# The same program at other SBUF addresses: buffers laid out anew, with a smaller dynamic DMA scratch

## The chip, the core and the metric

The kernel runs on one core of one Trainium2 chip. The metric is device time in microseconds (us) of one execution, and lower is better. TensorE (PE) multiplies, ScalarE (ACT) and VectorE (DVE) work elementwise, GpSimd (POOL) computes remainders here, and SyncE (SP) issues nearly all transfers. Buffers lie in SBUF, 128 partitions wide; an address below is a byte offset inside each partition. Products gather in eight PSUM banks.

## The reference, cut to what matters

A first transformer block and then two layers of a second one run on x of 512 tokens by 1024 channels, in float32.

```python
def reference(x, c, positions, w_mod, ...):
    x = first_block(x, c, positions, ...)      # modulation, gated delta rule (8 heads) and latent attention,
                                               # merged through w_o_dn, w_o_mla, w_out; then 16 experts
    return second_block(x, positions_2, ...)   # 2 layers of:

def second_block(...):
    for l in range(2):
        h = rmsnorm(x, mix_norm_g[l])
        x = x + mixing_layer(h, ...)           # short conv, differential attention, conformer conv
        h = rmsnorm(x, ffn_norm_g[l])
        x = x + swiglu(h, w_gate[l], w_up[l], w_down[l])   # hidden width 2816
    return rmsnorm(x, final_norm_g)

def expert_choice_ffn(h, ...):                 # 16 experts, 64 tokens each, hidden width 1024
    hid = silu(xe @ w_gate) * (xe @ w_up)
    ye = (hid @ w_down) * gate
```

## The kernel before

The program is one `build` function with a hand-written stream for each engine, joined by semaphores. Weights come in pieces of 1 MB, each an 8192-byte row in all 128 partitions.

**Buffers.** Nothing is allocated by a planner. `base` (line 72) is the first free SBUF byte rounded up to 64; each `Region` (from line 76) hands out offsets from `base`, one after the other, in steps of 32 bytes; `at` puts a tensor at a given offset, so that many names share one place. Ahead of the first free byte stand 97 bytes of constants and the dynamic DMA scratch, which is 16384 bytes unless the program says otherwise. So `base` is 16512, which is 8 x 2048 + 128. From `base` on stand eight ring buffers of 8192 bytes, `x`, `hT` and `xn` of 16384 each, then some 11 kB of small tensors, and then `ARENA` at 142048, in which every stage lays out its own tensors.

**Split matmuls.** The merge of the first block and all projections of the second block use float32 split in two rounded halves (`fp32r`): ACT rounds a piece of weights into `w_hi` (line 728), POOL subtracts to get `w_lo` (`remainder`, line 676), and the activations are split in the same way into pairs such as `hT_hi` and `hT_lo`. `mm3` then makes three matmuls of each product:

```python
def mm3(dst, a, b, start, stop, before=False):
    first = mm(dst, a[0], b[0], start=start, stop=False)   # line 1551, hi x hi
    mm(dst, a[0], b[1], start=False, stop=False)           # line 1555
    return mm(dst, a[1], b[0], start=False, stop=stop)     # line 1556
```

The first operand is the stationary one (128 x 128, brought in by a weight load); the second one moves through the array, 512 or 256 columns. In the profile a row `bank<-hT_lo,w_hi` names the moving operand first. Three users matter:

- `merge` (line 1563): weights stationary, moving operands `h_hi`/`h_lo`, `o_dn_hi`/`o_dn_lo` or `o_mla_hi`/`o_mla_lo`, 512 columns.
- `blocks2` (line 1855): weights stationary, `hT_hi`/`hT_lo` moving. It does gate and up of the feed-forward part and some input projections (also inside `fill2`, line 1961, between the steps of the attention). Moving width 512, or 256 while only half of the tokens are ready.
- `tokens2` (line 1881): `hT` or `yT` halves stationary, weights moving, 256 columns. The down projection of the feed-forward part is written in the same manner with `ffn_hi`/`ffn_lo` stationary and weights of 512 columns moving.

The other matmuls (delta rule, latent attention, `w_out`, experts) are plain float32. In the experts' stage `chunk_pair` (line 1796) waits for each piece in the ring.

**Where the operands lie before** (address, and address modulo 2048):

| tensor | address | mod 2048 | tensor | address | mod 2048 |
|---|---|---|---|---|---|
| w_lo0, w_hi1, w_lo1, w_hi0 (ring 0, 1, 2, 7) | 16512 to 73856 | 128 | o_dn_hi | 57472 | 128 |
| h_hi | 114816 | 128 | o_dn_lo | 142048 | 736 |
| h_lo | 98432 | 128 | o_mla_hi | 174816 | 736 |
| hT_hi | 98432 | 128 | o_mla_lo | 158432 | 736 |
| hT_lo | 204512 | 1760 | yT_hi | 114816 | 128 |
| ffn_hi, ffn_lo | 114816, 123008 | 128 | yT_lo | 154624 | 1024 |
| extra0 and 1; 2 and 3 | 98432 on; 198496 on | 128; 1888 | gt2_b; gt1_b, gfin_b | 133632; 225216, 221120 | 512; 1984 |

128 and 1024 are multiples of 64; 736 and 1760 leave 32 when divided by 64.

Of the kernel before, what the change touches and what calls it, by code (L numbers as in the profile page):

```python
# [7 lines left out]
F32 = mybir.dt.float32  # L8
I32 = mybir.dt.int32
F32R = mybir.dt.float32r  # L10
# [4 lines left out]
P = 128  # L15
SEQ, DM = 512, 1024
TT = SEQ // P
KD = DM // P
EPS, LN_EPS = 1e-6, 1e-5
HEADS, HD = 8, 128  # L20
# [13 lines left out]
PI_IN = 3.1415925  # L34

RING = 8
RAW = 4


# [2 lines left out]
N_OUT = N_LATENT + 3  # L42
# [18 lines left out]
def build(nc, A, out):  # L61
# [3 lines left out]
    def sem(name):  # L65
        if name not in sems:
            sems[name] = ctx.enter_context(nc.semaphore(name))
        return sems[name]

    with ctx:  # L70

        base = nc.sbuf_base + (-nc.sbuf_base) % 64
        top = nc.sbuf_usable_end

        def at(name, offset, shape, dt=F32):
            return nc.alloc_sbuf_tensor_at(name, shape, dt, offset=base + offset)

        class Region:
# [2 lines left out]
            def __init__(self, start, end):  # L81
                self.pos, self.end = start, end

            def __call__(self, name, shape, dt=F32):
                t = at(name, self.pos, shape, dt)
                self.pos += 4 * int(np.prod(shape[1:]))
                self.pos += (-self.pos) % 32
                assert self.pos <= self.end, (name, self.pos, self.end)
                return t

        everything = Region(0, (top - base) // 64 * 64)
        ring = [everything(f"ring{i}", [P, 2048]) for i in range(RING)]
        x = everything("x", [P, TT, DM])
        HT_AT = everything.pos
        hT = everything("hT", [P, KD, SEQ])
        XN_AT = everything.pos
        xn = everything("xn", [P, TT, DM])
        XN_END = everything.pos
        ident = everything("ident", [P, P])
        cols_a = everything("cols_a", [P, R_A])  # L100
        cols_l = everything("cols_l", [P, L_ROWS])
# [19 lines left out]
        ss = everything("ss", [P, 16])  # L121
        rms = everything("rms", [P, 16])
        rstd = everything("rstd", [P, 16])
        ARENA, ARENA_END = everything.pos, everything.end

        bank = [ctx.enter_context(nc.psum_tensor(f"bank{i}", [P, 512], F32)) for i in range(8)]


        r = Region(N_OUT % RING * 8192, RING * 8192)
        mod2_w = r("mod2_w", [P, KD, 512])  # L130
        mod2_part = r("mod2_part", [P, HEADS, 512])
        quarters = r("quarters", [P, P])
# [3 lines left out]
        r = Region(ARENA, ARENA_END)  # L136
# [47 lines left out]
        head_q = r("head_q", [P, 5, TT * 2])  # L184
        xr = Region(XN_AT, XN_END)
        decay = xr("decay", [P, 2, TT, P])
# [12 lines left out]
        r = Region(HEADW_AT, ARENA_END - 4096)  # L199
# [18 lines left out]
        pinv = r("pinv", [P, 2])  # L218
        pT = at("pT", XN_AT, [P, 2, TT, SEQ])
        r = Region(HEADW_AT, HEADW_AT + 16384)  # L220
# [2 lines left out]
        latent_diag = r("latent_diag", [P, 2, TT, P])  # L223


        o_dn_hi = at("o_dn_hi", (N_OUT + 2) % RING * 8192, [P, HEADS, SEQ], F32R)
        o_dn_lo = at("o_dn_lo", ARENA, [P, HEADS, SEQ], F32R)
        h_hi = at("h_hi", XN_AT, [P, KD, SEQ], F32R)
        h_lo = at("h_lo", HT_AT, [P, KD, SEQ], F32R)
        o_mla_hi = at("o_mla_hi", PARTS_1_AT, [P, HEADS, SEQ], F32R)  # L230
        o_mla_lo = at("o_mla_lo", HEADW_AT, [P, HEADS, SEQ], F32R)
        r = Region(PARTS_1_AT + 16384, MERGE_AT + 32768 + 1024)
# [5 lines left out]
        r = Region(ARENA, ARENA_END - 8192)  # L238
# [6 lines left out]
        asum = r("asum", [P, TT])  # L245
        gate_col = r("gate_col", [P, 1])
        ye = r("ye", [P, DM])
        ye_hi = r("ye_hi", [P, DM], F32R)
        xeT = r("xeT", [P, KD, P])
        hid = r("hid", [P, DM])  # L250
        hidT = r("hidT", [P, KD, P])
        ye_lo = r("ye_lo", [P, DM], F32R)
        scat_now = r("scat_now", [P, SEQ], F32R)
        slotT = r("slotT", [EXPERTS, SEQ])
        slotT_r = at("slotT_r", r.pos - 2048, [EXPERTS, SEQ], F32R)
        pair_sel = r("pair_sel", [EXPERTS, PAIRS, P])
# [1 line left out]
        top8 = r("top8", [EXPERTS, 8, 8])  # L258
        assert r.pos <= ARENA + 4 * FB * SEQ + 8192

        EXTRA_AT = ARENA + 56448
        extra = [at(f"extra{i}", HT_AT + 8192 * i if i < 2 else EXTRA_AT + 8192 * (i - 2), [P, 2048]) for i in range(EXTRA)]
        r = Region(EXTRA_AT + 16384, ARENA_END - 8192)
        work = r("work", [EXPERTS, 2, SEQ])
# [3 lines left out]
        r = Region(ARENA, ARENA_END - 8192)  # L268
# [11 lines left out]

        squares = at("squares", HT_AT, [P, TT, DM])
        r2 = Region(MERGE_AT + 32768 + 1024, ARENA_END - 4096)
        rows_2 = r2("rows_2", [L_ROWS, LAYERS, P])
        lam_in = r2("lam_in", [P, 4, LAYERS, 64])
        lam_p = r2("lam_p", [P, 2, LAYERS, 64])
        hT_hi = at("hT_hi", HT_AT, [P, KD, SEQ], F32R)
        yT_hi = at("yT_hi", XN_AT, [P, KD, SEQ], F32R)
        ffn_hi = at("ffn_hi", XN_AT, [P, 2, 2, SEQ], F32R)
        ffn_lo = at("ffn_lo", XN_AT + 8192, [P, 2, 2, SEQ], F32R)

        raw = [ring[(N_LAYER + i) % RING] for i in range(RAW)]
        w_hi, w_lo = [], []
        for i in range(2):
            slot = (N_LAYER + RAW + 2 * i) % RING
            w_hi.append(at(f"w_hi{i}", slot * 8192, [P, 2048], F32R))
            w_lo.append(at(f"w_lo{i}", (slot + 1) % RING * 8192, [P, 2048], F32R))
        r = Region(ARENA, ARENA + 4 * FB * SEQ)
        glu = r("glu", [P, 2, 30 + SEQ])
        conf = r("conf", [P, 2, SEQ])
        prod = r("prod", [P, 2, 2 + SEQ])  # L300
        YLO_AT = r.pos
        q2T = r("q2T", [P, 4, SEQ])
        k2T = r("k2T", [P, 4, SEQ])
# [14 lines left out]
        rot = [at(f"rot{i}", XN_AT + 4096 * (i + 1) if i < 3 else ARENA + 4 * FB * SEQ, [P, 2, 512]) for i in range(4)]  # L318
        r = Region(AFTER_FFN, ARENA_END - 8192)
        PARTS_AT = r.pos  # L320
        hT_lo = r("hT_lo", [P, KD, SEQ], F32R)
        yT_lo = at("yT_lo", YLO_AT, [P, KD, SEQ], F32R)
        rope_2 = at("rope_2", ARENA + 4 * FB * SEQ + 4096, [P, 2, SEQ])
        p2 = at("p2", ARENA + 4 * FB * SEQ, [P, 4, SEQ])
# [7 lines left out]

        raw_landed = [sem(f"raw_landed_{i}") for i in range(RAW)]
        hi_ready, lo_ready, parts_used = sem("hi_ready"), sem("lo_ready"), sem("parts_used")
# [77 lines left out]
        def parts_ready(eng, m, l):  # L412

            eng.wait_ge(lo_ready, MERGES + l * PER_LAYER + RAW + m + 1)

# [31 lines left out]
        def merge_raw(m):  # L447

            if m < 8:
                return m % 2, 16 * (m // 2 + 1)  # L450
            return m % RAW, 16 * ((4 if m % RAW < 2 else 0) + (m - 8) // RAW + 1)

# [5 lines left out]
        def _(sp):  # L458
# [65 lines left out]
            def load_merge(m):  # L524
# [5 lines left out]
                elif m >= 12:  # L530
                    sp.wait_ge(lo_ready, m - RAW + 1)
                elif m >= 10:
# [2316 lines left out]
```

How the kernel before makes its waits and increments, by code:

```python
        def reached(eng, name):  # L358
            eng.wait_ge(step[name], step_count[name])
# [31 lines left out]
        def in_turn(eng, name, turn):  # L392
            per_turn, place = turn_place[name]
            eng.wait_ge(once_a_turn[name], turn * per_turn + place)
# [7 lines left out]
        def expert_done(eng, pair, part):  # L403
            chunks = (8, 16, 24)[part] - (EXTRA if part and pair == 0 else 0)
            eng.wait_ge(chunk_used, ring_base(pair) + chunks)
# [1 line left out]
        def arrived(eng, n, it=0, per=0):  # L408
            eng.wait_ge(landed[n % RING], it * (16 * per // RING) + 16 * (n // RING + 1))
# [1 line left out]
        def parts_ready(eng, m, l):  # L412
            eng.wait_ge(lo_ready, MERGES + l * PER_LAYER + RAW + m + 1)
# [1 line left out]
        def parts_free(eng, m, l):  # L416
            eng.wait_ge(parts_used, MERGES + l * PER_LAYER + m + 1)
# [38 lines left out]
        @block.sync  # L457
# [1 line left out]
            def load(n, dst, src, it=0, per=0, slots=1):  # L459
                if slots and (n >= RING or per):
                    sp.wait_ge(chunk_used, it * per + (n - RING + slots))
                sp.dma_start(dst, src).then_inc(landed[n % RING], 16)
# [36 lines left out]
                src = w_mod[:, 2048:].rearrange("(k p) (h n) -> p k h n", p=P, h=HEADS)
                src = src[:, :, bass.ds(h, 1), :] if not isinstance(h, int) else src[:, :, h:h + 1, :]
                sp.dma_start(mod2_w[:].unsqueeze(2), src).then_inc(sem("mod2_w_in"), 16)
            sp.wait_ge(chunk_used, N_LATENT)
            load_mod2(0)
            sp.wait_ge(sem("qkv_done"), 3)
```

## Time and profile before

| what | value |
|---|---|
| runs | 2853.17, 2854.38, 2857.24 us |
| median | 2854.38 us |
| span of the profiled execution | 2853.2 us |
| PE busy | 2688.1 us, 94% |
| DVE, ACT, POOL busy | 996.5, 824.1, 784.2 us |
| mean DMA rate | 134 GB/s; 408 to 410 GB/s in the experts' stage |

For the profiled execution the trace gives the span alone, from the first to the last instruction, and it equals the lowest of the three runs: nothing that can be seen lies around it. Busy time of PE is counted with modelled ends, so that a matmul of 512 columns reads as 390 ns though the next one starts 227 ns later; what a matmul costs is read as the distance between starts, a window's length divided by the matmuls in it. A window's count holds those in flight at its edge too, one to three more than start in it.

### The profile page before, as it was taken

To read this page: it belongs to the slowest core of one execution; us is meant where nothing else is said; L and a number is where in the kernel's file an instruction comes from. 1 tells how busy PE (TensorE), PEld (TensorE's weight loads), DVE (VectorE), ACT (ScalarE), POOL (GpSimd) and SP (SyncE) were. 2 spreads that over 40 slices of the span, in tenths; PEclk is the share of its full clock that TensorE was granted. 3 is DMA by queue.
4 is the path that set the end of the run, shared out by engine and by line. 5 is a ranking of instruction groups with operands and counts; after the bars stand their busy time and mean duration, and the time that the engine had idled before them with its cause. 6 is when DMAs were issued, how large, how long until landed. Compare 5 with 4: busy or idle time off the path is not lost.

```text
span 2853.2 us, 35499 instructions
## 1 busy us (share of the span) xinstructions
PE 2688.1 (94%) x14496; PEld 2005.0 (70%) x14496; DVE 996.5 (35%) x1800; ACT 824.1 (29%) x1440; POOL 784.2 (27%) x633
## 2 busy tenths in 40 slices
PE   7999999999989996999999799999999999999998
PEld 4777777786447885444444398888888896988887
DVE  3555555532331224221211278520001497300012
ACT  3433333332333212100000124532222327322222
POOL 2222222220013410000000043344445442444444
PEclk8999999999999997999999999999999999999999
DMA  7211111102012323799999922123232221223231
GB/s 259 52 59 59 59 59 59 37 30 82 19 48 78 120 103 133 310 409 409 409 408 407 349 92 65 60 81 96 90 103 89 89 90 45 75 89 103 89 103 45
DMA packets 212565, 382.39 MB, mean 134 GB/s; under 512 B 10833, under 2 KB 145877, under 8 KB 211413
## 3 DMA queue, kind: packets, MB, share of 16 engines
q1 hardware_dynamic: 211088, 379.06, 37.3%
q8 instruction: 95, 1.56, 0.2%
q10 hardware_dynamic: 1349, 1.51, 0.2%
q14 instruction: 33, 0.27, 0.0%
HBM read 378.44 MB, written 2.10 MB: 133 GB/s over the span
## 4 chain that ended last, share of the span: by engine, by line
PE 70%; DMA 8%; issue 6%; PEld 5%; DVE 4%; ACT 3%; POOL 1%; DVEq 1%; PEldq 0%; SPq 0%; ACTq 0%; POOLq 0%
PE bank L1551 14%; PE bank L1555 14%; PE bank L1556 14%; PE bank L1811 7%; DMA ring<-in_w_up 4%; DMA ring<-in_w_gate 3%; PE bank L1756 2%; PE bank L1699 2%; PEld bank L1359 2%; PE bank L1419 2%; PE bank L1428 1%; PE bank L1605 1%; PE bank L1432 1%; PE bank L1622 1%; PE bank L1896 1%
## 5 line engine op out<-in xcount | busy, mean ns | idle before, releaser
L680 POOL TENSOR_TENSOR w_lo<-ring,w_hi 128x512 fp32r<-128x512 f32 x448 | 606.3, 1385 | 1496.0 <-ACT w_hi L728 1496.0
L728 ACT ACTIVATE w_hi<-ring 128x2048 fp32r<-128x2048 f32 (+1 forms) x114 | 215.0, 1886 | 677.2 <-PE bank L1551 677.1
L1551 PE MATMUL bank<-hT_hi,w_hi 128*128 128x512 f32 (+1 forms) x928 | 357.6, 385 | 3.2 <-DVE hT_lo L2603 1.6
L1555 PE MATMUL bank<-hT_lo,w_hi 128*128 128x512 f32 (+1 forms) x928 | 350.1, 377 | 0.0
L1556 PE MATMUL bank<-hT_hi,w_lo 128*128 128x512 f32 (+1 forms) x928 | 348.2, 375 | 0.0
L1811 PE MATMUL bank<-ring,xeT 128*64 128x512 f32 x992 | 225.4, 596 | 31.4 <-DMA ring<-in_w_gate 18.4
L1551 PEld LDWEIGHTS bank<-hT_hi,w_hi 128*128 128x128 f32 x928 | 174.4, 188 | 37.9 <-DVE conv_acc L2701 2.4
L1556 PEld LDWEIGHTS bank<-hT_hi,w_lo 128*128 128x128 f32 x928 | 174.6, 188 | 37.3
L1555 PEld LDWEIGHTS bank<-hT_lo,w_hi 128*128 128x128 f32 x928 | 173.9, 187 | 32.5 <-issue 1.0
L1811 PEld LDWEIGHTS bank<-ring,xeT 128*64 128x64 f32 x992 | 76.6, 136 | 156.4 <-issue 153.9
L2794 DVE TENSOR_TENSOR ffn_hT<-ffn_sg,bank 128x512 f32<-128x512 f32 x44 | 30.2, 688 | 423.0 <-PE bank L1556 423.0
L1325 PE MATMUL bank<-hT,head_w 128*128 128x512 f32 x336 | 156.9, 593 | 0.0
L1551 PE MATMUL bank<-w_hi,ffn_hi 128*128 128x512 f32 x352 | 137.1, 390 | 0.0
L1555 PE MATMUL bank<-w_lo,ffn_hi 128*128 128x512 f32 x352 | 137.0, 389 | 0.0
L1556 PE MATMUL bank<-w_hi,ffn_lo 128*128 128x512 f32 x352 | 136.9, 389 | 0.0
L655 POOL TENSOR_TENSOR intra<-decay,tri 128x512 f32<-128x512 f32 x16 | 20.3, 1271 | 381.1 <-ACT decay L851 381.1
L1811 PE MATMUL bank<-ring,hidT 128*64 128x512 f32 x512 | 112.3, 594 | 3.9 <-DMA ring<-in_w_down 3.0
L2653 DVE SCALAR_TENSOR_TENSOR conf<-glu,cols_l,conf 128x512 f32<-128x512 f32 x120 | 112.9, 971 | 6.6 <-issue 1.3
L1551 PE MATMUL bank<-w_hi,hT_hi 128*128 128x256 f32 x384 | 109.0, 284 | 1.7 <-ACT q2T L1133 1.7
L1556 PE MATMUL bank<-w_hi,hT_lo 128*128 128x256 f32 x384 | 108.3, 282 | 0.0
L1555 PE MATMUL bank<-w_lo,hT_hi 128*128 128x256 f32 x384 | 108.0, 281 | 0.0
L2788 DVE TENSOR_TENSOR ffn_lo<-ffn_hT,ffn_hi 128x1024 fp32r<-128x1024 f32 x22 | 31.8, 1446 | 198.1 <-ACT ffn_hi L728 198.1
(490 smaller groups left out, 4896.3 us busy)
## 6 DMA issues: line engine op xcount, KB each, us to landing
ring<-in_w_gate SPq DMA_DIRECT2D x86, 1024.0 KB, 9.0
ring<-in_w_down SPq DMA_DIRECT2D x86, 1024.0 KB, 14.1
ring<-in_w_up SPq DMA_DIRECT2D x82, 1024.0 KB, 14.1
ring<-in_w_in SPq DMA_DIRECT2D x33, 1024.0 KB, 5.5
head_w<-in_w_in SPq DMA_DIRECT2D x32, 512.0 KB, 5.4
mod_w<-in_w_mod SPq DMA_DIRECT2D x8, 2048.0 KB, 8.3
ring<-in_w_out SPq DMA_DIRECT2D x12, 1024.0 KB, 5.0
ring<-in_w_mod SPq DMA_DIRECT2D x8, 1024.0 KB, 15.7
```

Of the source, the lines that this page charges most:

```text
L680: last = pool.tensor_tensor(w_lo[m % 2][:, cs], src[:, cs], w_hi[m % 2][:, cs].bitcast(F32), ALU.subtract)
L728: return act.activation(dst, src, ACT.Copy)
L1325: last = mm(bank[0 if s == 1 else 1][:], head_w[:, k, s * HD:(s + 1) * HD], hT[:, k, :], start=k == 0, stop=k == KD - 1)
L1359: last = mm(bank[2][:, t * P:(t + 1) * P], hT[:, k, t * P:(t + 1) * P], head_w[:, k, 3 * HD:4 * HD], start=k == 0, stop=k == KD - 1)
L1419: last = mm(bank[4][:, tiles[t]], solve_S[:, lv % 2, t, :], solve_X[:, t, :], start=True, stop=True)
L1551: first = mm(dst, a[0], b[0], start=start, stop=False)
L1555: mm(dst, a[0], b[1], start=False, stop=False)
L1556: return mm(dst, a[1], b[0], start=False, stop=stop)
L1699: last = mm(bank[t % 2 * 2 + c // 2][:, c % 2 * 256:(c % 2 + 1) * 256], mT[:, k, t * P:(t + 1) * P], kview(N_OUT + c)[:, k, :], start=k == ...
L1756: last = mm(bank[4 + half][:, k % 4 * P:(k % 4 + 1) * P], xn[:, t, k * P:(k + 1) * P], onehot[:, t, pair * P:(pair + 1) * P], start=t == 0 ...
L1811: last = mm(bank[banks + hf][a * 64:a * 64 + 64, :], lhs[:, 2 * j + kk, a * 64:a * 64 + 64], chunk[a][:, kk, hf * 512:(hf + 1) * 512], sta ...
L2653: stt(conf[:, b, :], glu[:, b, j:j + SEQ], w, conf[:, b, :], ALU.mult, ALU.add)
```

## The change

No instruction, wait or transfer is changed. Tensors get other addresses:

- The dynamic DMA scratch is 1024 bytes and not 16384. The first free byte goes from 16481 to 1121, `base` from 16512 to 1152.
- The small tensors come first, from 1152 to 12000. The ring follows at 12288, a multiple of 2048 (`RING_AT` replaces the 0 from which ring offsets were counted), then `x`, `hT`, `xn`, and `ARENA` at 126976, all of them on multiples of 2048.
- A `line` argument lets a tensor start on a multiple of 2048: `ye_hi`, `ye_lo`, `scat_now`, `hT_lo`, and the position `YLO_AT`. `EXTRA_AT` moves by 896 bytes relative to `ARENA`.

After it every tensor of the table above, but for `gt2_b` (3584, 1536 modulo 2048) and `gt1_b` and `gfin_b` (unmoved), stands at 0 modulo 2048. Ring, `x`, `hT` and `xn` all move by the same 4224 bytes. `hT_lo` goes from 204512 to 190464, `o_dn_lo` to 126976, `o_mla_lo` to 143360, `o_mla_hi` to 159744, `yT_lo` to 141312.

```diff
+LINE = 2048
-            def __call__(self, name, shape, dt=F32):
+            def __call__(self, name, shape, dt=F32, line=32):
+                self.pos += -(base + self.pos) % line
                 t = at(name, self.pos, shape, dt)
...
-        ring = [everything(f"ring{i}", [P, 2048]) for i in range(RING)]
-        x = everything("x", [P, TT, DM])
-        (hT and xn likewise)
         ident = everything("ident", [P, P])
...
         rstd = everything("rstd", [P, 16])
+        ring = [everything(f"ring{i}", [P, 2048], line=LINE) for i in range(RING)]
+        RING_AT = everything.pos - RING * 8192
+        x = everything("x", [P, TT, DM])
+        (hT and xn likewise)
...
-        ye_hi = r("ye_hi", [P, DM], F32R)
+        ye_hi = r("ye_hi", [P, DM], F32R, line=LINE)
...
-        EXTRA_AT = ARENA + 56448
+        EXTRA_AT = ARENA + 57344
...
-            w_hi.append(at(f"w_hi{i}", slot * 8192, [P, 2048], F32R))
+            w_hi.append(at(f"w_hi{i}", RING_AT + slot * 8192, [P, 2048], F32R))
...
+        r.pos += -(base + r.pos) % LINE
         YLO_AT = r.pos
...
-        hT_lo = r("hT_lo", [P, KD, SEQ], F32R)
+        hT_lo = r("hT_lo", [P, KD, SEQ], F32R, line=LINE)
...
-    nc = _bacc.Bacc("TRN2", target_bir_lowering=False, num_devices=1)
+    nc = _bacc.Bacc("TRN2", target_bir_lowering=False, num_devices=1, dynamic_dma_scratch_size=1024)
```

## Rows read from the trace of the kernel before

**Rows 1.** The page: the span, engines, and 40 slices in time.

```profile
span 2853.2 us, 35499 instructions
...
PE 2688.1 (94%) x14496; PEld 2005.0 (70%) x14496; DVE 996.5 (35%) x1800; ACT 824.1 (29%) x1440; POOL 784.2 (27%) x633
...
PE   7999999999989996999999799999999999999998
...
DMA  7211111102012323799999922123232221223231
```

**Rows 2.** The page's chain that ended last, by line.

```profile
PE bank L1551 14%; PE bank L1555 14%; PE bank L1556 14%; PE bank L1811 7%; DMA ring<-in_w_up 4%; DMA ring<-in_w_gate 3%; PE bank L1756 2%; PE bank L1699 2%; PEld bank L1359 2%; PE bank L1419 2%; PE bank L1428 1%; PE bank L1605 1%; PE bank L1432 1%; PE bank L1622 1%; PE bank L1896 1%
```

**Rows 3.** Groups of instructions, shapes apart, PE: busy and mean (modelled ends).

```profile
L1555 PE MATMUL bank<-hT_lo,w_hi 128*128 128x512 f32 x800 | 314.3, 393 | 0.0
...
L1555 PE MATMUL bank<-w_lo,ffn_hi 128*128 128x512 f32 x352 | 137.0, 389 | 0.0
...
L1555 PE MATMUL bank<-w_lo,hT_hi 128*128 128x256 f32 x384 | 108.0, 281 | 0.0
...
L1555 PE MATMUL bank<-w_lo,yT_hi 128*128 128x256 f32 x256 | 72.2, 282 | 0.0
...
L1555 PE MATMUL bank<-h_lo,w_hi 128*128 128x512 f32 x128 | 49.9, 390 | 0.0
...
L1555 PE MATMUL bank<-hT_lo,w_hi 128*128 128x256 f32 x128 | 35.8, 280 | 0.0
...
L1555 PE MATMUL bank<-o_mla_lo,w_hi 128*128 128x512 f32 x64 | 25.3, 395 | 0.0
L1555 PE MATMUL bank<-o_dn_lo,w_hi 128*128 128x512 f32 x64 | 25.3, 395 | 0.0
```

**Rows 4.** Windows of PE alone: stretch, length, busy (matmuls), clock, DMA share, GB/s.

```profile
888.54:904.86 16.32, 16.32 (x74) 1.00 0.33 106
904.86:915.95 11.09, 11.09 (x49) 1.00 0.31 91
993.15:1004.36 11.21, 11.21 (x49) 1.00 0.30 97
...
1657.77:1660.59 2.82, 2.82 (x26) 1.00 0.01 3
1663.45:1666.27 2.82, 2.82 (x26) 1.00 0.79 225
1680.22:1717.36 37.14, 37.14 (x314) 1.00 0.27 86
1835.85:1864.44 28.59, 28.59 (x243) 1.00 0.36 111
1898.63:2120.50 221.87, 221.87 (x962) 1.00 0.30 95
...
1898.63:1909.72 11.09, 11.09 (x49) 1.00 0.32 96
1909.72:1920.82 11.10, 11.10 (x50) 1.00 0.30 94
```

**Rows 5.** The timeline of PE in gate and up, then in down: start, length.

```profile
1926.36 0.40 PE L1551 MATMUL bank<-hT_hi,w_hi 128*128 128x512 f32 x1
...
1927.06 0.40 PE L1551 MATMUL bank<-hT_hi,w_hi 128*128 128x512 f32 x1
...
2141.72 0.39 PE L1551 MATMUL bank<-w_hi,ffn_hi 128*128 128x512 f32 x1
...
2142.40 0.39 PE L1551 MATMUL bank<-w_hi,ffn_hi 128*128 128x512 f32 x1
```

**Rows 6.** The attention of a layer, 1752 to 1829: windows, then line 1551 there.

```profile
1752.00:1829.00 77.00, 71.93 (x394) 53.33 (x393) 53.00 (x111) 54.23 (x151) 18.57 (x15) 1.00 0.14 46
...
L1551 PE MATMUL bank<-hT_hi,w_hi x48: 393/397/797, 1753.6 to 1821.8; 128*128 128x512 f32 x48
```

**Rows 7.** The chain around `w_out` and in the experts' stage: start, us, what.

```profile
1039.47 20.75 PE bank L1699 x96
...
1255.30 13.02 DMA ring<-in_w_gate
...
1272.51 16.28 DMA ring<-in_w_up
```

**Rows 8.** The DMA view of two windows, 665.0 to 666.5 and 1195 to 1620.

```profile
DMA packets 173, 0.62 MB, mean 415 GB/s; under 512 B 21, under 2 KB 21, under 8 KB 173
...
q1 hardware_dynamic: 173, 0.62, 101.7%
...
DMA packets 45003, 173.73 MB, mean 409 GB/s; under 512 B 2639, under 2 KB 2639, under 8 KB 44986
```

**Rows 9.** The page's DMA queues: packets, MB, share of 16 engines.

```profile
q1 hardware_dynamic: 211088, 379.06, 37.3%
q8 instruction: 95, 1.56, 0.2%
q10 hardware_dynamic: 1349, 1.51, 0.2%
q14 instruction: 33, 0.27, 0.0%
```

**Rows 10.** Engines other than PE: line or tile, durations min/median/max or mean ns.

```profile
L680 POOL TENSOR_TENSOR w_lo<-ring,w_hi x448: 1260/1297/2274, 806.3 to 2830.8; 128x512 fp32r<-128x512 f32 x150
...
L651 POOL TENSOR_TENSOR solve_S<-l_neg,level_mask 128x512 f32<-128x512 f32 x56 | 72.9, 1307 | 70.1 <-PE bank L1419 44.2 <-DVE l_neg L2266 20.4 <-DVE solve_Y L2273 5.5
...
L2581 DVE TENSOR_TENSOR ye_lo<-ye,ye_hi 128x512 fp32r<-128x512 f32 x16 | 10.8, 692 | 0.3
...
L2476 DVE TENSOR_TENSOR x<-x,upd 128x512 f32<-128x512 f32 x8 | 5.5, 692 | 0.7
```

More of the change, by code:

```diff
@@ L91, in build @@
         everything = Region(0, (top - base) // 64 * 64)
-        ring = [everything(f"ring{i}", [P, 2048]) for i in range(RING)]
-        x = everything("x", [P, TT, DM])
[L94 to L98, printed above, removed]
         ident = everything("ident", [P, P])
@@ L123, in build @@
         rstd = everything("rstd", [P, 16])
+        ring = [everything(f"ring{i}", [P, 2048], line=LINE) for i in range(RING)]
+        RING_AT = everything.pos - RING * 8192
+        x = everything("x", [P, TT, DM])
+        HT_AT = everything.pos
+        hT = everything("hT", [P, KD, SEQ])
+        XN_AT = everything.pos
+        xn = everything("xn", [P, TT, DM])
+        XN_END = everything.pos
         ARENA, ARENA_END = everything.pos, everything.end
         bank = [ctx.enter_context(nc.psum_tensor(f"bank{i}", [P, 512], F32)) for i in range(8)]
-        r = Region(N_OUT % RING * 8192, RING * 8192)
+        r = Region(RING_AT + N_OUT % RING * 8192, RING_AT + RING * 8192)
         mod2_w = r("mod2_w", [P, KD, 512])
@@ L223, in build @@
         latent_diag = r("latent_diag", [P, 2, TT, P])
-        o_dn_hi = at("o_dn_hi", (N_OUT + 2) % RING * 8192, [P, HEADS, SEQ], F32R)
+        o_dn_hi = at("o_dn_hi", RING_AT + (N_OUT + 2) % RING * 8192, [P, HEADS, SEQ], F32R)
         o_dn_lo = at("o_dn_lo", ARENA, [P, HEADS, SEQ], F32R)
@@ L251, in build @@
         hidT = r("hidT", [P, KD, P])
-        ye_lo = r("ye_lo", [P, DM], F32R)
-        scat_now = r("scat_now", [P, SEQ], F32R)
+        ye_lo = r("ye_lo", [P, DM], F32R, line=LINE)
+        scat_now = r("scat_now", [P, SEQ], F32R, line=LINE)
         slotT = r("slotT", [EXPERTS, SEQ])
@@ L294, in build @@
             slot = (N_LAYER + RAW + 2 * i) % RING
-            w_hi.append(at(f"w_hi{i}", slot * 8192, [P, 2048], F32R))
-            w_lo.append(at(f"w_lo{i}", (slot + 1) % RING * 8192, [P, 2048], F32R))
+            w_hi.append(at(f"w_hi{i}", RING_AT + slot * 8192, [P, 2048], F32R))
+            w_lo.append(at(f"w_lo{i}", RING_AT + (slot + 1) % RING * 8192, [P, 2048], F32R))
         r = Region(ARENA, ARENA + 4 * FB * SEQ)
```

## The prediction

> **What bounds the kernel now.** I read the page first: PE is busy in every slice but a few, and DMA is near its limit only in slices 17 to 22, the experts' stage [rows 1]. The chain that ended last says the same: 42% of it are the three lines of the split matmul `mm3`, and only a few per cent are transfers for the experts [rows 2]. So outside the experts' stage, time is the number of matmuls times the distance between their starts, and an edit that changes no instruction can act only through that distance, through the duration of other engines' work where it is on the path, or through the transfers.
>
> So I read distances, for equal work at different addresses. Windows in which PE does one form only give them [rows 4], with the one to three matmuls that only overlap an edge taken off the count. 512 moving columns:
>
> - `h_hi`, `h_lo` moving, all operands at 128 modulo 2048: 16.32 us for 72 matmuls, 226.7 ns each. The down projection, at 128 too, repeats after 0.68 us for three, the same 227 ns [rows 5].
> - gate and up, `hT_lo` at 1760: 221.87 us for 960, 231.1 ns. The triple takes 0.69 to 0.70 us in the timeline [rows 5].
> - `o_dn_lo` at 736: 11.09 us for 48, 231.0 ns.
> - `o_mla_hi` and `o_mla_lo`, both at 736: 11.21 us for 48, 233.5 ns.
>
> The shape, the clock (1.00) and the DMA share (0.30 to 0.33) are alike. What differs is where moving operands stand: the fast forms have all at 128 (a multiple of 64, and the same remainder as the weights), the slow forms have one or two at 32 modulo 64. That is a difference of 4.4 ns for one such operand in the triple, 6.8 ns for both. It is also a difference of position: all the slow ones lie above 131072, all the fast ones below. The trace before can't part the two, which makes the main rival.
>
> **The change, part by part.** *Smaller scratch.* Nothing in the trace uses it: the queues that move data are the hardware-driven ones of SP and ACT [rows 9]. Cost and gain 0; it makes room for the rounding and moves everything down.
>
> *Ring, x, hT, xn.* They move together by 4224 bytes, so among themselves their offsets stay. I take `h`, down and the experts' reads at 0. What could change is the remainder 128 becoming 0 (second rival).
>
> *hT_lo.* It comes to the remainder of `hT_hi` and the weights, the situation of `h_lo`. Per triple 3 x (231.1 - 226.7) = 13.3 ns. There are 800 triples of 512 columns [rows 3]. 48 of them lie in each of the two attention stretches [rows 6], where PE works 71.93 of 77 us and is repeatedly held by the softmax steps. So 704 are in back-to-back stretches: 704 x 13.3 ns = 9.4 us. For the 96 others 96 x 13.3 ns = 1.3 us if all of it counts, 0 if the softmax chain takes it back; PE's share of that stretch is high, yet each step there waits for ACT and DVE, so I take half, 0.6 us.
>
> *o_dn_lo, o_mla_hi, o_mla_lo.* 64 triples each [rows 3]: 64 x 13.3 ns = 0.9 us, and 64 x 3 x 6.8 ns = 1.3 us. PE is saturated in the merge.
>
> *256 columns.* Three forms: `hT` moving, early and late tokens, 2.82 us for 24, 117.5 ns; `tokens2` on `hT`, 37.14 us for 312, 119.0 ns; `tokens2` on `yT`, 28.59 for 240, 119.1 ns [rows 4]. `hT_lo` at 1760 and `yT_lo` at 1024 as stationary operands give the same 119, so the remainder of the stationary operand shows no cost; and with `hT_lo` moving, 256 columns show no surcharge either. I take 0. Bounds: the 640 `tokens2` triples [rows 3] fall to 117.5, 1920 x 1.5 ns = 2.9 us gained; or the 128 others rise to 119.0, 384 x 1.5 = 0.6 us lost.
>
> *Plain float32.* 96 of 256 columns in 20.75 us, 216.1 ns each [rows 7], with `ring` at 128 and `mT` at 736. That is 0.84 ns a column, nearly double the split form's 0.44, so it takes in data at about half the rate; a mixed layout shows no surcharge that I can find. 0.
>
> *Other engines.* POOL's remainder with both inputs at equal remainders takes 1297 ns at the median, its `solve_S` at 736 and 1248 takes 1307; DVE takes 692 ns for a subtraction at 1632 and 692 with `x` at 128 and `upd` at 736 [rows 10]. Addresses make no difference there, and none of them is the bound in the long stretches. 0.
>
> *Transfers.* The experts' stage waits for pieces: 13.02 us and 16.28 us in one pair of experts [rows 7], with 409 GB/s moved [rows 8]. So there what PE gains is lost in the wait, and a faster transfer would count in full. The ring rows start at 128 modulo 256. The row for a 256-aligned destination is `gt2_b`, in 665.0 to 666.5: 415 GB/s, a window of 152 large packets, against 409 GB/s over 425 us [rows 8]. Were all of that 1.5% due to alignment, 425 x 0.015 = 6.2 us would go. But the window is short and its end effects are of that size, so I take 0 and keep 6.2 us as a bound. The Trainium skill (DMA: Bandwidth & Descriptors, How a descriptor splits into AXI transactions) says that a transaction starts on a 256-byte boundary, and that a descriptor which doesn't start there fetches unused bytes. Applied to 4096 bytes at 128, that is an estimate of 4 beats in 132, 3%, some 13 us of the stage; the rows bear out at most half of it, and the page speaks of reads while here the SBUF side is written.
>
> **Sum.** 9.4 + 0.6 + 0.9 + 1.3 = 12.2 us. The profiled execution spans 2853.2 us, 1.2 below the median of the runs, with nothing seen around it. Span after: 2841.0; median 2854.4 - 12.2 = 2842.2 us. Own range: half the effect in gate and up costs 4.7 us, the 256-column forms reach 2.9 us the other way: 2838 to 2847.
>
> **Rivals.**
>
> *Position, not alignment.* The 4.4 ns goes with an operand above 131072. After the change `hT_lo`, `o_mla_hi`, `o_mla_lo` and most of `o_dn_lo` are still above it: no change, 2854. For it: the clean split by position. Against: `o_dn_lo` near 142000 and `hT_lo` near 204500 give the same 231, and the weights in ring 0 and ring 7, 57 kB apart, give alternate pieces one distance (the last two windows of [rows 4], one piece each). The same time comes out if the surcharge is in the order of the operands. The Trainium skill (SBUF — State Buffer, the note on SBUF cachelines) names lines of 16 bytes; by that rule offsets 32, 64 or 128 all start a line and this change does nothing. The rows show 226.7 and 231.1 for what it calls alike, but can't say why. Chance 0.14.
>
> *The remainder 128 costs too.* The fast 226.7 is itself above half of a float32 matmul's time per column, 216.1 ns for 512 columns. If that 10.6 ns is due to starting at 128 rather than 0, it goes everywhere: (800 + 352 + 128 + 64 + 64) x 3 = 4224 matmuls x 10.6 ns = 44.8 us, and 768 x 3 = 2304 of 256 columns x (118.8 - 108.1) = 24.7 us. With the 12.2 that is 2773. Against it: the excess is about 11 ns at 256 and at 512 columns alike, so it belongs to each matmul with its weight load and not to the bytes read; and early tokens (slices that don't cross a multiple of 2048) and late ones (slices that do) take the same 2.82 us [rows 4], so crossing costs nothing. Chance 0.08.
>
> *Transfers gain by alignment.* 2842.2 - 6.2 = 2836. For: 415 against 409. Against: as above. Chance 0.06, on top of the forecast.
>
> *Everything in step is worse.* With all large tensors at 0 modulo 2048, the reads of PE, the writes of ACT, POOL and the transfers start at equal remainders. If that costs PE the 4.4 ns wherever it now takes 226.7 ns, and `hT_lo` keeps its own, then down and `h`, (352 + 128) x 3 = 1440 matmuls, pay 6.3 us: 2860.7. It decides in the first down block: 24 matmuls over 5.5 us in place of 5.44. Against: ring, `x`, `hT` and `xn` are in step already, and these are the fast forms. Chance 0.06.
>
> **How the numbers follow.** Forecast 0.66, with transfers 0.06, position 0.14, remainder 128 0.08, in step 0.06. Leaving out the last two and taking the others whole gives 2836 to 2855. A measurement of this kernel tells no change from one of 0.2%, 5.7 us. Faster: 0.66 + 0.06 + 0.08 = 0.80; within: 0.14; slower: 0.06.
>
> **What would show it.** In the changed profile, the window of gate and up: 960 matmuls in 217.6 us, triples repeating after 0.68 us; the merge with `o_mla` at 226.7 ns; down, plain float32 and the experts unchanged, 409 GB/s. The attention stretches each shorten by 0 to 0.6 us. Gate and up at 231.1 would speak for position, the first rival; down at 216 for the second. The prediction goes wrong if the surcharge belongs to position, or if a form that is fast now loses its speed at remainder 0.

## The result and the profile after

The changed kernel takes 2836.78 us (2830.01 to 2840.0, 5 runs), the kernel before on the same chip 2855.56 us (2853.17 to 2857.24, 5 runs). The ratio is 0.9927 [0.9916, 0.9938], that is 0.6 to 0.8% faster. Forecast were 12.2 us and at the lower end of the range 2838 us; the medians differ by 18.8 us, and the changed kernel lies below the range. A second comparison, further down, gives 0.9933 [0.9916, 0.995], 20.2 us.

The page after answers [rows 1] and [rows 2]. Source lines are four higher than before: the three matmuls of `mm3` are 1555, 1559 and 1560.

```profile
span 2834.9 us, 35499 instructions
...
PE 2681.1 (95%) x14496; PEld 2010.8 (71%) x14496; DVE 993.6 (35%) x1800; ACT 824.8 (29%) x1440; POOL 782.0 (28%) x633
...
PE   7999999999989996999999899999999999999998
...
DMA  7111111102012423799999921123232221223231
```

It looks almost the same: the same number of instructions, PE busy nearly throughout, DMA full in the same slices. A shortening that is spread over 14496 matmuls does not show in tenths. Since both programs issue the same matmuls in the same order, the k-th matmul of one can be set against the k-th of the other. That is the view that finds the time (us from the first instruction, worked out from the two traces):

```
k-th matmul  before   after   after-before  gained or lost since the line above
4500          858.9   858.1      -0.76      first block
5600         1109.6  1106.8      -2.77      -2.0  merge
8000         1654.9  1641.3     -13.56     -10.8  experts
9000         1800.9  1787.8     -13.07      +0.5  layer 1: projections
9400         1858.7  1848.6     -10.16      +2.9  layer 1: end of attention
9560         1878.2  1868.0     -10.12       0.0
11050        2208.1  2193.6     -14.51      -4.4  layer 1: gate and up
12700        2460.7  2446.8     -13.91      +0.6  layer 2: mixing
14200        2778.2  2760.0     -18.25      -4.3  layer 2: gate and up
14495        2845.1  2826.9     -18.25       0.0
```

So three lines hold the story: the merge and gate and up do what was forecast (2.0 of 2.2 us, 8.7 of 9.4 us); the experts' stage, forecast at 0, gives 10.8 us; and the mixing parts lose about 4 us, forecast as a gain of 0.6.

The windows of PE alone in the changed kernel, for the same matmuls as [rows 4] and the `w_out` part of [rows 7]: `h` 72, `o_dn` 48, `o_mla` 48, plain float32 96, `hT` moving with 256 columns 24 early and 24 late, `tokens2` on `hT` 312 and on `yT` 240, gate and up 960.

```profile
887.73:904.05 16.32, 16.32 (x73) 1.00 0.33 103
904.05:914.93 10.88, 10.88 (x49) 1.00 0.30 88
991.09:1001.97 10.88, 10.88 (x49) 1.00 0.26 91
1036.79:1057.51 20.72, 20.72 (x99) 1.00 0.24 99
1644.30:1647.18 2.88, 2.88 (x27) 1.00 0.00 0
1650.06:1652.94 2.88, 2.88 (x27) 1.00 0.80 282
1666.72:1704.16 37.44, 37.44 (x315) 1.00 0.27 85
1825.52:1854.32 28.80, 28.80 (x242) 1.00 0.36 110
1888.53:2106.13 217.60, 217.60 (x962) 1.00 0.30 97
```

Every window of 512 columns now divides to 226.7 ns: 10.88 us / 48, 217.60 / 960. The windows of 256 columns divide to 120.0 ns, where before they gave 117.5 to 119.1: 2.88 for 2.82, 37.44 for 37.14, 28.80 for 28.59. That is a loss, and the prediction had it at 0.

The DMA view of the experts' stage (1190 to 1605), which answers to the second window of [rows 8]:

```profile
DMA packets 45105, 174.11 MB, mean 420 GB/s; under 512 B 2651, under 2 KB 2651, under 8 KB 45087
...
q1 hardware_dynamic: 45087, 173.83, 102.3%
```

The queue is as full as before, 102.3% of sixteen engines, but moves 420 GB/s and not 409. The chain there still alternates between PE and pieces that are late, with shorter waits than the 13.02 and 16.28 us of [rows 7]:

```profile
1250.77 11.96 DMA ring<-in_w_gate
...
1266.93 15.69 DMA ring<-in_w_up
```

Where the 2.9 us of the first layer's attention went is seen in windows of PE, the second of them the one that matters (stretch, length, busy and matmuls, granted clock, DMA share, GB/s):

```profile
1796.00:1798.00 2.00, 0.78 (x4) 1.00 0.00 0
1798.50:1805.00 6.50, 5.72 (x18) 0.50 0.01 3
1805.50:1809.00 3.50, 3.50 (x18) 1.00 0.71 213
```

The granted clock is 0.50, the lower of its two levels, 1.2 GHz. The timeline of PE shows matmuls 0.43 us apart in it, where [rows 5] has 0.23, and the pauses of PE beside it:

```profile
1797.22 0.92 PE L1929 MATMUL bank<-k2T,q2T 64*128 64x384 f32 x4 [1.73 <-ACT p L1154]
...
1798.79 0.63 PE L1559 MATMUL bank<-hT_lo,w_hi 128*128 128x512 f32 x1
1799.22 0.63 PE L1560 MATMUL bank<-hT_hi,w_lo 128*128 128x512 f32 x1
1800.63 0.80 PE L1555 MATMUL bank<-hT_hi,w_hi 128*128 128x512 f32 x1 [0.78 <-DVE conv_acc L2705]
```

Before, the same place has the same two pauses, and the clock stays at 1.00:

```profile
1810.29 0.92 PE L1925 MATMUL bank<-k2T,q2T 64*128 64x384 f32 x4 [1.67 <-ACT p L1150]
...
1813.11 0.50 PE L1551 MATMUL bank<-hT_hi,w_hi 128*128 128x512 f32 x1 [0.78 <-DVE conv_acc L2701]
```

```profile
1806.00:1813.00 7.00, 4.67 (x26) 1.00 0.00 1
```

So PE pauses in both, first for a step of the softmax (ACT), then for one of the convolution (DVE), and only in one of the two does the clock fall.

### The profile page after: what moved, and what is told of

Same layout as the page of the kernel before. It is cut to its first block, busy times and chain, and to the rows that moved or that the text cites. A ratio compares the mean times of both kernels' runs of the same rounds, so it can differ in the third digit from the quotient of the medians.

```text
span 2834.9 us, 35499 instructions
## 1 busy us (share of the span) xinstructions
PE 2681.1 (95%) x14496; PEld 2010.8 (71%) x14496; DVE 993.6 (35%) x1800; ACT 824.8 (29%) x1440; POOL 782.0 (28%) x633
## 4 chain that ended last, share of the span: by engine, by line
PE 70%; DMA 8%; issue 7%; PEld 5%; DVE 4%; ACT 3%; POOL 1%; DVEq 1%; PEldq 0%; SPq 0%; ACTq 0%; POOLq 0%
PE bank L1555 14%; PE bank L1560 14%; PE bank L1559 14%; PE bank L1815 7%; DMA ring<-in_w_up 4%; DMA ring<-in_w_gate 3%; PE bank L1760 2%; PE bank L1703 2%; PEld bank L1363 2%; PE bank L1423 2%; PE bank L1432 1%; PE bank L1609 1%; PE bank L1436 1%; PE bank L1626 1%; PE bank L1900 1%
```

## The experiments

Eleven runs, in three groups, the first two of them with the kernels as they are; each time is compared with the kernel before on the same chip. Theory A of the first group: the layout itself does it, in two separate ways, on the matmuls through their operands and on the transfers through their destination. Rivals: B, the smaller scratch; C, the chip in one run.

### Group 1: is it real, and which of the two parts is it?

**The kernel before, unchanged.** 

> The kernel before, unchanged, for a second profile. If the slower transfers of the experts' stage belong to the layout (theory A) or to the size of the scratch (theory B), this profile shows them again: 409 GB/s in the stage, 4096-byte packets spread over 159 to 171 ns, 2855 us. If they belong to the state of the chip in one run (theory C), this profile may as well show 420 GB/s and 159 ns, and the time of both kernels would wander by some 10 us.

Measured: 2855.78 us, ratio 1.0003 [0.999, 1.0015].

**The changed kernel, unchanged.** 

> The changed kernel, unchanged, on the same chip as the other three. A and B: 420 GB/s in the experts' stage again and 2834 to 2838 us. C: the stage may show 409 GB/s, and then the time is near 2846 us. Gate and up at 226.7 ns a matmul in every case.

Measured: 2835.34 us, ratio 0.9933 [0.9916, 0.995]. The result repeats, and so does its profile: 420 GB/s, 226.7 and 120.0 ns, and the lower clock at the end of the first layer's attention. That all this belongs to the chip in one run (C) can be set aside. Between the two profiles of the same kernel the first 300 us differ by 1.3 us here and by 2.3 us for the kernel before; so the first block's -0.76 above is no finding.

**The scratch alone.**

```diff
-    nc = _bacc.Bacc("TRN2", target_bir_lowering=False, num_devices=1)
+    nc = _bacc.Bacc("TRN2", target_bir_lowering=False, num_devices=1, dynamic_dma_scratch_size=1024)
```

This moves every tensor down by 15360 bytes, a multiple of 256, and changes no remainder modulo 256. 

> Before, with the scratch at 1024 bytes and nothing else: all tensors move down by 15360 bytes, ring at 1152 modulo 2048 (128 modulo 256 as before), hT_lo still 32 modulo 64. A: no change, 409 GB/s, 2855 us. B: 420 GB/s in the experts' stage and about 2844 us. Gate and up stay at 231.1 ns by remainder modulo 64; o_dn_lo now lies at 126688 and partly below 131072, hT_lo at 189152.

Measured: 2857.26 us, ratio 1.0004 [0.9995, 1.0014]. The smaller scratch, and a move that keeps all remainders, do nothing.

**The kernel before, 128 bytes higher.** The ring, `x`, `hT` and `xn` come to 256 modulo 2048; what stands between the operands of a matmul is as before.

```diff
-        base = nc.sbuf_base + (-nc.sbuf_base) % 64
+        base = nc.sbuf_base + (-nc.sbuf_base) % 64 + 128
...
-        EXTRA_AT = ARENA + 56448
+        EXTRA_AT = ARENA + 56416
```

> Before, with every tensor 128 bytes higher (the two extra buffers 96): the ring, x, hT and xn at 256 modulo 2048, all offsets among the tensors kept, hT_lo still 32 modulo 64, scratch 16384. A, if a multiple of 256 is what the transfers need: 420 GB/s in the experts' stage and about 2844 us, with gate and up still at 231.1 ns. A, if they need more than 256: 409 GB/s. B: 409 GB/s, 2855 us.

Measured: 2845.74 us, ratio 0.9971 [0.9961, 0.9981]: half of the gain with no matmul changed. Its gate and up, 960 matmuls, and its DMA view of 1200 to 1570:

```profile
1887.52:2109.39 221.87, 221.87 (x962) 1.00 0.30 95
```

```profile
DMA packets 40208, 155.21 MB, mean 419 GB/s; under 512 B 2361, under 2 KB 2361, under 8 KB 40192
```

221.87 us is the 231.1 ns of before to the last digit, and the rate is 419 GB/s. Set matmul against matmul with the unchanged kernel before of this group, it gains 10.6 us between the 5500th and the 8000th and nothing behind them. The two effects are apart.

### Group 2: which remainder, and must operands be aligned or agree?

**One low half out of step.** In the changed kernel `hT_lo` stands at 32 modulo 2048 in layer 1 and at 64 in layer 2, `yT_lo` at 64.

```diff
-        hT_lo = r("hT_lo", [P, KD, SEQ], F32R, line=LINE)
+        LO_AT = r.pos + -(base + r.pos) % LINE
+        hT_los = [at("hT_lo", LO_AT + 32, [P, KD, SEQ], F32R), at("hT_lo1", LO_AT + 64, [P, KD, SEQ], F32R)]
...
-        r.pos += -(base + r.pos) % LINE
+        r.pos += -(base + r.pos) % LINE + 64
         YLO_AT = r.pos
```

> The changed kernel (2835.3 us on this measure) with three tensors moved off the multiples of 2048: the low half of the activations is at 32 modulo 2048 in the first layer and at 64 in the second, and yT_lo at 64. It parts what the 512-column matmuls want of their moving operands. Theory 64: each must start on a multiple of 64 bytes; then gate and up take 231.1 ns a matmul in the first layer and 226.7 in the second, and the time rises by 4.4 to 4.7 us, to about 2840, plus what the clock does in the first layer's attention. Theory same remainder: all operands must agree modulo 2048 (or 128); then both layers take 231.1 and the time rises by about 9 us, to 2844. For the 256-column matmuls: if their 120.0 ns (119.1 before) comes from all operands standing at one remainder, those on yT fall back to 119.1 in both layers and those on hT too; if it comes from the hi halves or the weights at 0, they stay at 120.0. The fall would be worth 640 x 3 x 0.9 ns = 1.7 us.

Measured: 2841.62 us, ratio 0.9954 [0.9938, 0.9971]. Windows: `tokens2` on `hT` (312), on `yT` (240), gate and up of layer 1 (960), and 720 matmuls of gate and up in layer 2.

```profile
1665.29:1702.21 36.92, 36.92 (x314) 1.00 0.27 87
1820.52:1848.78 28.26, 28.26 (x242) 1.00 0.36 112
1882.91:2105.31 222.40, 222.40 (x961) 1.00 0.29 95
2488.57:2655.61 167.04, 167.04 (x721) 1.00 0.30 95
```

222.40 / 960 is 231.7 ns, and 167.04 / 720 is 232.0: an operand on a multiple of 64 is as slow as one on 32. The theory of 64-byte starts falls; that of the same remainder stands. The time lies between the two expectations, 2840 and 2844 us, and decides nothing by itself. `tokens2` goes the other way: 28.26 / 240 is 117.8 ns, faster than before and after. Its clock was low in the attention of layer 2 instead of layer 1.

**Everything 128, 64 or 32 bytes higher.** All large tensors keep one common remainder, which is no longer 0. The diff is that of the first kernel; the two others have 64 and 32 in the place of 128.

```diff
+OFF = 128
...
-        base = nc.sbuf_base + (-nc.sbuf_base) % 64
+        base = nc.sbuf_base + (-nc.sbuf_base) % 64 + OFF
...
-                self.pos += -(base + self.pos) % line
+                self.pos += -(base + self.pos - OFF) % line
```

128: 

> The changed kernel with every tensor 128 bytes higher, so that the ring, x, hT and xn stand at 128 modulo 2048 as before the change, and all operands keep one remainder. Theory 256 (a transfer gains by a destination on a multiple of 256 bytes): the experts' stage falls back from 420 to 409 GB/s and lasts 10.6 us longer, gate and up stay at 226.7 ns; the time is about 2846. Rival (the rate follows from the ring's place or from the small tensors ahead of it): the rate stays at 420 and the time at 2835. The 256-column matmuls stay at 120.0 ns if one common remainder makes them slow, and fall to 119.1 or 117.8 if the remainder 0 does.

64: 

> The same with 64 bytes. Theory 256: a packet of 4096 bytes ends and starts inside a 256-byte block as it does at 128, so 409 GB/s again and about 2846 us. Rival (half a block is worse or better than a quarter): the rate is clearly another one, 400 or 415. Matmuls at 226.7 ns, as 64 is a multiple of 64; were 128 needed, all 4224 matmuls of 512 columns would take up to 6.8 ns more, 28.7 us.

32: 

> The same with 32 bytes, so that all operands agree in their remainder and none is on a multiple of 64. Theory 64 (absolute): every 512-column matmul takes 233.5 ns, as those on o_mla did before the change: 4224 x 6.8 ns = 28.7 us less some 1 us hidden in the attention; with 409 GB/s in the experts' stage the time is about 2873. Theory same remainder: they stay at 226.7 ns and the time is about 2846.

Measured: 2847.51 us, 0.9972 [0.9963, 0.9982]; 2845.77, 0.9968 [0.9957, 0.9979]; 2846.85, 0.9969 [0.9958, 0.9979]. All three land near the 2846 of the theories of 256 bytes for transfers and of the same remainder for matmuls, and the one with 32 nowhere near the 2873 of absolute alignment. The windows of the kernel with 32 bytes are `o_dn` (48), `o_mla` (48) and gate and up (960):

```profile
906.80:917.68 10.88, 10.88 (x49) 1.00 0.29 81
993.84:1004.72 10.88, 10.88 (x49) 1.00 0.29 88
1900.96:2118.56 217.60, 217.60 (x961) 1.00 0.31 97
```

All 226.7 ns with no operand on a multiple of 64: what counts for the matmuls is agreement. The DMA views (1200 to 1570) of the kernel with 128, then 64, then 32 bytes:

```profile
DMA packets 39189, 151.23 MB, mean 409 GB/s; under 512 B 2312, under 2 KB 2312, under 8 KB 39174
```

```profile
DMA packets 39191, 151.24 MB, mean 409 GB/s; under 512 B 2313, under 2 KB 2313, under 8 KB 39175
```

```profile
DMA packets 39175, 151.24 MB, mean 409 GB/s; under 512 B 2298, under 2 KB 2298, under 8 KB 39159
```

409 GB/s at 32, 64 and 128 modulo 256; 419 and 420 at 0. For the transfers it is the absolute address of the destination that counts, and how far it is off does not matter. The single packets of 4096 bytes in the traces say the same (ns, 1st, 50th and 90th percentile of 56320):

```
destination modulo 256     0 (after)       0 (before + 128)   128 (before)    64              32
                           159 159 159     159 159 159        159 160 171     159 162 167     159 162 166
```

### Group 3: modulo what, and a version made of it

**`hT_lo` further off.** As in group 2, with the offsets by norm (mixing, feed-forward of layer 1; of layer 2) and `yT_lo`: first 512, 256, 128, 128 and 128; then 256, 512, 1024, 1024 and 512.

```diff
+        LO_BY = (512, 256, 128, 128)
+        hT_los = [at(f"hT_lo_{n}", LO_AT + LO_BY[n], [P, KD, SEQ], F32R) for n in range(4)]
```

> The changed kernel with the low half of the activations further from the remainder that the other operands share: at 512 in the first layer's mixing, 256 in its feed-forward part, 128 in the second layer's mixing and feed-forward part; yT_lo at 128. It asks modulo what the operands must agree. If modulo 128, every form reads as in the changed kernel, 226.7 and 120.0 ns. If modulo 256, gate and up take 226.7 in the first layer and 231 to 232 in the second. If modulo 2048, both take 231 to 232. The 256-column forms go the other way: 120.0 where the operands agree, 117.7 to 119.2 where they don't; before the change yT_lo stood 896 bytes off, a multiple of 128, and took 119.2, which speaks against modulo 128.

> The same with 256 in the first layer's mixing, 512 in its feed-forward part, 1024 in the second layer's, and yT_lo at 512. If the operands must agree modulo 512, gate and up take 226.7 ns in both layers; if modulo 1024, the first layer takes 231 to 232 and the second 226.7; if modulo 2048, both take 231 to 232.

Each ran once, so only the windows are used: 2838.31 us and 2832.85 us, spans 2836.3 and 2830.8. The first kernel's gate and up at 256 (960), at 128 (720), and `tokens2` with `yT_lo` at 128 (240):

```profile
1885.75:2103.35 217.60, 217.60 (x962) 1.00 0.30 97
2487.16:2651.96 164.80, 164.80 (x721) 1.00 0.30 96
1822.97:1851.56 28.59, 28.59 (x243) 1.00 0.37 111
```

The second kernel's at 512 and at 1024:

```profile
1884.39:2101.99 217.60, 217.60 (x962) 1.00 0.30 97
2483.84:2647.04 163.20, 163.20 (x721) 1.00 0.31 97
```

256, 512 and 1024 are as good as 0: 226.7 ns. 128 gives 228.9. For 512 columns the operands must agree modulo 256.

**Each low half where its matmuls want it.** `hT_lo` is 64 bytes off in the mixing parts (256 columns mostly) and in step in the feed-forward parts; `yT_lo` is 64 off.

```diff
+        LO_BY = (64, 0, 64, 0)
...
-        r.pos += -(base + r.pos) % LINE
+        r.pos += -(base + r.pos) % LINE + 64
```

> The changed kernel with each low half where its matmuls want it: yT_lo and the low half of the activations of the mixing layers (256 columns mostly) 64 bytes off the shared remainder, that of the feed-forward parts (512 columns) on it. If what the runs so far showed for each form adds up: 640 triples x 3 x 2.2 ns = 4.2 us less, 96 triples of 512 columns in the attention that may lose 96 x 3 x 5.5 ns = 1.6 us, and the attention of the first layer with the clock at 1.2 GHz for a while or without it, 2.8 us. So 2831 to 2833 on this measure, 2828 if that stretch keeps its clock. Rival (the 256-column matmuls are hidden behind another limit): 2835 to 2837.

Measured: 2830.02 us (2828.34 to 2831.46), ratio 0.9912 [0.9895, 0.9928]. Against the kernel before it is the fastest of all. The medians of the changed kernel are 2835 to 2837 us, on other chips; the intervals of the ratios overlap, so that it is faster than the changed kernel, by some 5 us, is a reading of medians and not shown by the times alone. Of these, 2.8 us are the clock in the attention, which stays high here. Windows: `tokens2` on `hT` (312) and `yT` (240), gate and up.

```profile
1667.27:1704.02 36.75, 36.75 (x314) 1.00 0.28 87
1822.21:1850.47 28.26, 28.26 (x242) 1.00 0.34 112
1884.64:2102.24 217.60, 217.60 (x961) 1.00 0.30 97
```

These three forms run at the best distance seen for them, 117.8, 117.8 and 226.7 ns. The fourth does not: `hT` moving with 256 columns takes 120.0 ns in layer 1, from start to start over the 24 matmuls from 1644.78 us on, though `hT_lo` stands 64 off there. Set matmul against matmul with the changed kernel of group 1, the mixing part of layer 1 (8000th to 9500th) is 4.3 us shorter, 2.8 of them by the clock (what the same stretch gains in the kernel 128 bytes higher, whose matmuls take what those of the changed one take), and that of layer 2 (11500th to 13000th) 1.5 us. So the offsets give 1.5 + 1.5 = 3.0 us net. The expectation has 4.2 for the 256-column forms and up to 1.6 lost on the 96 triples of 512 columns, whose `hT_lo` is out of step here (those ahead of the first attention take 232.7 ns). The second kernel of the pair above, on the same chip, says the same: it keeps its clock too and has all these forms in step, and from the 4500th matmul on it takes 3.2 us longer.

## Why the prediction was wrong, point by point

**The step that failed: the transfers.** "I take 0 and keep 6.2 us as a bound." The mechanism stood in the prediction, as a rival; its term in the sum was mis-sized. The stage gave 10.8 us between matmuls 5600 and 8000, and the shift by 128 bytes alone 10.6 us. The rates agree: 425 us x (1 - 409 / 420) = 11.1 us. The bound was too low since it came from one window of 152 large packets into `gt2_b`. Its 415 GB/s came at a queue share of 101.7%, less than the stage's 102.3%, so the window was not quite full, and its rate was no upper bound of what alignment gives. The estimate of 13 us, which the prediction worked out from the Trainium skill (DMA: Bandwidth & Descriptors, How a descriptor splits into AXI transactions) and held to be borne out "at most half", came nearer, and the 256-byte boundary that the page states for reads is where the runs put it for the destination. The page's count of beats does not carry over as it was used: by it a start at 32 would cost a quarter of one at 128, and the runs show 409 GB/s for both. With this term at 11 in place of 0 the forecast would have been 2831, and the 4.6 us by which the mixing parts miss their term lead from there to 2836. The rival's own 2836 us was met by luck: its 6.2 us were 4.6 too few, and the mixing parts gave back as much.

**The chances.** "Transfers gain by alignment" had 0.06, against 0.66 for a forecast without it, although its only row pointed that way and nothing but the shortness of the window spoke against it. With even odds the range would have reached further down.

**The matmuls of 512 columns: right.** 226.7 ns in every window of the split form, 8.7 us in gate and up for the 9.4 forecast, 2.0 for 2.2 in the merge. The prediction left two readings open, "a multiple of 64, and the same remainder as the weights". It is the second: agreement modulo 256. By distance from agreement, one operand of the triple off: 231.7 ns at 32, 232.0 at 64, 231.1 at 96 (`hT_lo` before), 228.9 at 128. Both moving halves 96 off the weights: 233.5 (`o_mla` before), so it does not help that the two moving operands agree with each other. Nor is the surcharge in the one matmul that reads the odd operand. In gate and up before, the mean distance to the next start is 233.3 ns after line 1551, 230.8 after 1555, which reads `hT_lo`, and 229.2 after 1556. Why PE gains by agreement is shown by no run.

**Position: rejected.** `hT_lo` at 190464 is above 131072 and takes 226.7 ns; the scratch alone, 15360 bytes lower, changed nothing.

**The remainder 128 costs too: rejected.** Common remainders 0, 32, 64 and 128 all give 226.7 ns, and plain float32 215.9 (20.72 us / 96) for 216.1.

**Everything in step is worse: rejected for 512 columns, which the rival priced; true for 256, which it did not.** In step a 256-column matmul takes 120.0 ns. In `tokens2`, where the activations are stationary, it takes 118.3 with the low half 32 off, 117.8 at 64, 119.0 at 96 and 119.1 at 128. With `hT` moving the offset alone does not decide: 117.5 at 96 before, but 120.0 in layer 1 at 32 and at 64. The bound of the step "256 columns", 0.6 us lost, left out that the 640 `tokens2` triples, at 119.0, could get slower as well. 1920 x 0.95 ns + 384 x 2.5 ns = 2.8 us, of which about 1.1 us shows in the cumulative table; that the rest lies under waits of the attention is not shown.

**The attention: wrong in sign.** Half of 1.3 us was forecast as a gain. Layer 1 lost 2.9 us to the lower clock. It occurs there in both profiles of the changed kernel and in that with 32 bytes, in layer 2 in two others (`hT_lo` at 32 and 64, and the first sweep), and in neither in the other eight profiles. The pauses of PE are the same before and after, to 0.1 us. What decides whether they lower the clock was not found: no experiment here sets it, and that the moment at which PE reaches them matters is only a guess.

**Parts that add up.** Transfers alone (before + 128) give -9.8 us, operands alone (changed + 128) -8.7 us, each against the kernel before on its chip; the sum, -18.6, is within the scatter of the -20.2 measured for both in group 1.

## What to carry to other kernels

Put each buffer that transfers fill at a high rate on a multiple of 256 bytes; that was 2.6% of the rate here, and it counts in full wherever the next matmul waits for a piece. Then look at the distance between the starts of matmuls of each form and choose the remainders modulo 256 of their operands by it. Here that was equal for 512 moving columns, and the low half 64 off where it was stationary under 256; one tensor can have two addresses if it serves both forms. Only split float32 matmuls with 128 x 128 weights were tried. When a row suggests an effect and its size is only known from a short window, take the effect as likely and the size as open, upwards too; and compare two traces matmul by matmul, since a page in tenths shows none of this.

## What the runs showed that was not expected

- SBUF addresses change the distance of matmuls by up to 3%, in opposite directions for two widths: operands out of step take 226.7 ns up to 233.5 for 512 columns, and 120.0 ns down to 117.8 for 256 in `tokens2`.
- The rate in the experts' stage, 409 or 420 GB/s, depends on whether the destinations are multiples of 256, and is the same 32, 64 and 128 bytes off.
- PE's granted clock fell to 0.50 beside pauses of 1.7 and 0.8 us that left it at 1.00 in eight of the thirteen profiles. Each fall cost 2.7 to 2.9 us, a tenth of a per cent of the kernel.
- 15 kB less scratch, and every address moved with it, changed nothing (1.0004 [0.9995, 1.0014]).
